# Six weight sets instead of four in an expert loop, its first rows turned earlier, and a tail that reads its two accumulators separately

## The reference

```python
def moe(x, p):                       # 1032 tokens, 64 experts, top 6
    scores = jax.nn.sigmoid(jnp.einsum('nd,de->ne', x, p['w_router']).astype(F32))
    _, e_idx = lax.top_k(scores + p['router_bias'].astype(F32), TOP_K)
    w = jnp.take_along_axis(scores, e_idx, axis=1)
    w = w / jnp.sum(w, axis=-1, keepdims=True) * ROUTED_SCALE
    ...
    shared = swiglu(x, p['w_sh_gate'], p['w_sh_up'], p['w_sh_down'])
    return (routed + shared).astype(x.dtype)   # routed: sum over 6 experts of w * swiglu

x = layer_norm(DN_ALPHA * x + moe(x), ln2_g, ln2_b)
```

## Time and profile before

| | us |
|---|---|
| median of 3 runs | 2173.97 (2173.53 to 2175.95) |
| the profiled execution, device time | 2176.85 |
| its span in the trace | 2175.0 |
| first matmul of the expert loop | 1400.71 |
| first matmul of the last full pair (blocks 62 and 63) | 2088.45 |
| first matmul of the tail | 2134.93 |
| TensorE busy | 2078.7 (96%) |

### The profile page before, as it was taken

The page is one execution under the profiler, slowest core; times in us unless marked ns, Lnnn a source line. Parts: engine busy times, 40 slices in busy tenths (PEclk is TensorE's granted clock), DMA queues, the critical chain, the costliest instruction groups (busy, mean ns, idle before and its releaser), DMA issues.

```text
span 2175.0 us, 28927 instructions
## 1 busy us (share of the span) xinstructions
PE 2078.7 (96%) x10068; PEld 1304.5 (60%) x10068; DVE 1052.0 (48%) x2141; ACT 622.7 (29%) x1326; POOL 634.7 (29%) x782
## 2 busy tenths in 40 slices
PE   7998999899999999999999999999999999999996
PEld 5454665678788888888885556444444444444442
DVE  3225888754476684454444558533333233232335
ACT  1124777555335571121112220011111111111114
POOL 0002665301000000000000000357676656666562
PEclk9998999999999999999999999999999999999998
DMA  8202000347321111022303123699999999999956
GB/s 242 98 1 107 2 2 2 118 154 286 110 54 39 39 36 44 20 59 78 96 21 133 68 89 140 259 351 362 365 359 358 346 354 350 352 363 341 351 166 240
DMA packets 139888, 378.33 MB, mean 174 GB/s; under 512 B 27747, under 2 KB 88887, under 8 KB 112507
## 3 DMA queue, kind: packets, MB, share of 16 engines
q1 hardware_dynamic: 111795, 291.67, 36.5%
q0 software_dynamic: 27120, 84.40, 13.3%
q10 hardware_dynamic: 864, 0.79, 0.1%
HBM read 342.53 MB, written 58.00 MB: 184 GB/s over the span
## 4 chain that ended last, share of the span: by engine, by line
PE 75%; DMA 13%; DVE 5%; ACT 3%; issue 2%; POOL 0%; SPq 0%; DVEq 0%; POOLq 0%; ACTq 0%
PE PS L1277 19%; PE PS L1507 15%; DMA arena<-in_w_exp_down 11%; PE PS L1518 6%; PE PS L917 5%; PE PS L1416 5%; PE PS L806 4%; PE PS L1400 3%; PE PS L950 2%; PE PS L1092 2%; PE PS L987 2%; PE PS L811 2%; PE PS L1580 2%; PE PS L857 1%; PE PS L1455 1%
## 5 line engine op out<-in xcount | busy, mean ns | idle before, releaser
L1277 PE MATMUL PS<-arena 128*128 128x258 f32 x2352 | 514.7, 381 | 3.0 <-DVE arena L2384 2.7
L1507 PE MATMUL PS<-arena 128*128 128x512 f32 x1040 | 462.3, 598 | 30.1 <-issue 14.1
L1277 PEld LDWEIGHTS PS<-arena 128*128 128x128 f32 x2352 | 445.6, 190 | 70.2 <-issue 3.2
L1590 ACT ACTIVATE arena<-PS 128x258 f32<-128x258 f32 (+12 forms) x525 | 237.3, 464 | 656.2 <-PE PS L1277 238.1
L1507 PEld LDWEIGHTS PS<-arena 128*128 128x128 f32 x1040 | 193.7, 191 | 275.0 <-issue 270.0
L2762 POOL DMA_INDIRECT arena<-x_rows,tokall x276 | 278.0, 1007 | 170.6 <-DVE tokall L2615 101.6
L1518 PE MATMUL PS<-arena 128*128 128x512 f32 x520 | 233.9, 592 | 0.5 <-ACT arena L1590 0.5
L2746 POOL MEMSET arena<- 128x2 f32 x1 | 0.1, 100 | 739.8 <-PE PS L1416 739.8
L2636 DVE TENSOR_TENSOR arena<-PS,arena 128x256 f32<-128x256 f32 x65 | 27.6, 425 | 347.7 <-issue 175.6
L1518 PEld LDWEIGHTS PS<-arena 128*128 128x128 f32 x520 | 96.4, 191 | 109.2 <-issue 108.6
L2630 DVE STREAM_TRANSPOSE arena<-arena 128x1024 f32<-128x1024 f32 x67 | 135.7, 2026 | 40.1 <-DMA arena<-x_rows,tokall 39.0
(11 more groups left out here) (344 smaller groups left out, 2266.1 us busy)
## 6 DMA issues: line engine op xcount, KB each, us to landing
arena<-in_w_exp_gate SPq DMA_DIRECT2D x65, 1024.0 KB
arena<-in_w_exp_up SPq DMA_DIRECT2D x65, 1024.0 KB
arena<-in_w_exp_down SPq DMA_DIRECT2D x65, 1024.0 KB
arena<-in_w_in SPq DMA_DIRECT2D x34, 512.0 KB, 5.2
expert_rows<-arena SPq DMA_DIRECT2D x16, 512.0 KB
arena<-expert_rows SPq DMA_DIRECT2D x6, 1024.0 KB, 12.2
arena<-in_x_prompt SPq DMA_DIRECT2D x9, 512.0 KB, 5.0
arena<-x_rows,tokall POOLq DMA_INDIRECT x276
```

What stands on the lines that cost most here:

```text
L1277: ins = mm(PS[:, bank, 0:QT], lhs[:, l0 + k, :], right[:, r0 + k, c0:c0 + QT], start=first and k == 0, stop=k == kh - 1, skip_group_check= ...
L1507: ins = mm(PS[:, 2 + s, :].rearrange("p (h n) -> p h n", h=2), xgT[:, s, k, :], up_w[w][:, :, k, :], start=k == 0, stop=k == KT - 1)
L1590: return fn(out, in_, ACT.Copy)
```

## The change

It has three parts.

**Six weight sets.** Block b uses place b mod 6. The new places lie where constants, routing tables and LN1's vectors lay, whose last readers are done by then. Two of the six (3 and 4) have no room for the last eighth of their up matrix next to the rest, so that piece has a place elsewhere (`up_last`), its own DMA of 1 KB for each partition, and TensorE reads the last slice of gate and up with a longer step (`last_chunk`). The loop on TensorE and SyncE takes three pairs a turn instead of two, with two pairs behind it; a load now waits for the block three pairs earlier. Set 3 is loaded ahead of the loop, set 4 after the last addition, and set 5 where set 3 was.

**Rows of block 0.** VectorE turns the rows of block 0 ahead of the ninth shared addition (8 rows), and TensorE starts block 0 after eight additions.

**Tail.** SyncE reads the second accumulator as soon as `yd1` says that block 63 has been added, and TensorE puts its part of the first four tiles into PSUM; the first accumulator follows after `yd0` into a buffer of its own (`rows1`), and TensorE adds it. In the last full pair GpSimd issues both scatters ahead of the gathers that follow.

The diff, cut to what matters:

```diff
-        up_w = [wex[:, :, 0], wex[:, :, 1], at(4000, 2, KT * DE).rearrange("p h (k n) -> p h k n", k=KT), at(12256, 2, KT * DE).rearrange("p h (k n) -> p h k n", k=KT)]
-        down_w = [wexd[:, 0], wexd[:, 1], at(8096, 2, D), at(16352, 2, D)]
-        s_set = [sem(f"wset{w}") for w in range(4)]
+        NSET, NLATE = 6, 4
+        up_w = [wex[:, :, 0], wex[:, :, 1], gate_up_at(4000), gate_up_at(23536), gate_up_at(P), gate_up_at(12256)]
+        up_last = {3: 29760, 4: 29760 + DE}
+        down_w = [wexd[:, 0], wexd[:, 1], at(8096, 2, D), at(10144, 2, D), at(21472, 2, D), at(16352, 2, D)]
...
-        other = at(30784, NT, D)
+        other = at(12256, NT, D)
+        rows1 = at(30784, NT, D)
...
+            def up_in(w, x):
+                rows = a["w_exp_up"][bass.ds(x, 1), :, :].rearrange("u (p k) n -> (u p) (k n)", p=P)
+                if w in up_last:
+                    sp.dma_start(up_w[w][:, 1, 0:KT - 1].rearrange("p k n -> p (k n)"), rows[:, 0:(KT - 1) * DE]).then_inc(s_set[w], 16)
+                    sp.dma_start(at(up_last[w], DE), rows[:, (KT - 1) * DE:KT * DE]).then_inc(s_set[w], 16)
+                else:
+                    sp.dma_start(up_w[w][:, 1].rearrange("p k n -> p (k n)"), rows).then_inc(s_set[w], 16)
...
+            up_in(3, 3)
             sp.wait_ge(sem("shT_done"), 2)
             down_in(0, 0)
             sp.wait_ge(sem("sh_mm"), 4)
             gate_up_in(2, 2)
             down_in(2, 2)
+            down_in(3, 3)
+            sp.wait_ge(sem("hot_done"), NT)
+            gate_in(3, 3)
             sp.wait_ge(sem("table_step"), 4)
             down_in(1, 1)
...
+            sp.wait_ge(sem("ix1"), 2)
+            sp.wait_ge(sem("set_out"), 16 * NT + 32)
+            gate_up_in(4, 4)
+            sp.wait_ge(sem("shd_mm"), NT)
+            down_in(4, 4)
             sp.wait_ge(sem("x1_out"), 32 * NT)
-            gate_up_in(3, 3)
-            down_in(3, 3)
+            gate_up_in(5, 5)
+            down_in(5, 5)
...
+            def pair_in(r, p):
+                experts = [sp.value_load(blke[0:1, bass.ds(r * NSET + 2 * p + s, 1)], min_val=0, max_val=NE - 1) for s in range(2)]
+                for s, x in enumerate(experts):
+                    sp.wait_ge(sem(f"gu_mm{s}"), r * 3 + p - 1)
+                    gate_up_in(2 * p + s, x)
+                for s, x in enumerate(experts):
+                    sp.wait_ge(sem("y_mm"), r * NSET + 2 * p + s - 3)
+                    down_in(2 * p + s, x)
...
+            sp.wait_ge(sem("yd1"), landed[1])
+            rows_back(other, acc_rows[1], OTHER_IN)
+            sp.wait_ge(sem("yd0"), landed[0])
+            rows_back(rows1, acc_rows[0], Y_IN)
...
-            pe.wait_ge(sem("acc_done"), NT)
+            pe.wait_ge(sem("acc_done"), NT - 1)
...
+            with pe.Fori(0, NE // NSET) as r:
+                for p in range(3):
+                    full(r, p)
+            for p in range(2):
+                full(NE // NSET, p)
...
+            pe.wait_ge(*OTHER_IN[0])
+            for t in range(4):
+                if t == 2:
+                    pe.wait_ge(sem("y_ev"), blocks + 2)
+                    pe.wait_ge(sem("y_ev2"), blocks + 2)
+                sum_of(t, other, False)
             for t in range(NT):
...
+                if t == 4:
+                    pe.wait_ge(*OTHER_IN[4])
+                if t >= 4:
+                    pe.wait_ge(sem("centred"), t - 3)
+                    sum_of(t, other, False)
+                if t in Y_IN:
+                    pe.wait_ge(*Y_IN[t])
+                E.do(sum_of(t, rows1, True), sem("summed"))
...
-            for s in range(2):
-                rows_T(0, s)
+            rows_T(0, 0)
+            shared_add(NT - 1)
+            E.settle()
+            dve.nop().then_inc(sem("y_ev2"), 2)
+            rows_T(0, 1)
+            blocks = dve.value_load(nblk[0:1, 0:1], min_val=NE, max_val=NBLK)
...
+            for s in range(2):
+                rows_out(NE // 2 - 1, s, s)
+            for s in range(2):
+                rows_after_next(NE // 2 - 1, s, 2 + s)
```

More of the change, by code:

```diff
@@ L458, in build @@
         s_const = s_load[4]
-        Y_IN = {m: (s_load[k], (48, 96, 48, 64, 112)[k]) for k, m in enumerate((0, 1, 2, 4, 6))}
+        Y_IN = {m: (s_load[k], (32, 80, 672, 528, 80)[k]) for k, m in enumerate((0, 1, 2, 4, 6))}
         s_x = [sem(f"x_in{k}") for k in range(4)]
         s_xin = s_x[2:4]
+        OTHER_IN = {0: (s_xin[0], 128 + 80 + 16), 4: (s_xin[1], 128 + 64 + 32)}
         s_wta = sem("wta_in")
@@ L761, in spare_in @@
                 down_in(w, x)
[L763 to L771, removed]
+            def pair_in(r, p):
[6 more added lines that the diff above has]
+                    down_in(2 * p + s, x)
+            with sp.Fori(1, NE // NSET) as r:
+                for p in range(3):
+                    pair_in(r, p)
+            for p in range(2):
+                pair_in(NE // NSET, p)
             for lo, hi in SPARE:
@@ L782, in _, with rows_back @@
                                         spare_in(q, 3)
-            for s in range(2):
[L785 to L788, removed]
+            def rows_back(to, rows, groups):
+                for (m, (s, _)), hi in zip(groups.items(), list(groups)[1:] + [NT]):
                     top = min(hi, NT - 1)
@@ L1556, in spare @@
                 down(s, w, 1).then_inc(sem("y_mm"), 1)
-            with pe.Fori(0, NE // 4) as q:
-                for p in range(2):
-                    full(q, p)
+            with pe.Fori(0, NE // NSET) as r:
+                for p in range(3):
+                    full(r, p)
+            for p in range(2):
+                full(NE // NSET, p)
             for lo, hi in SPARE:
@@ L1571, in _, with sum_of @@
                                         spare(q, 3)
-            for t in range(NT):
[L1573 to L1581, removed]
+            def sum_of(t, rows, last):
+                n = rows_of(t)
+                for c in range(2):
+                    ins = mm(PS[0:n, 2 * (t % 4) + c, :], ident[0:n, 0:n], rows[0:n, t, c * 512:(c + 1) * 512], start=not last, stop=last, skip_group_check=True)
+                return ins
+            pe.wait_ge(*OTHER_IN[0])
[4 more added lines that the diff above has]
+                sum_of(t, other, False)
+            for t in range(NT):
+                if t == 4:
[6 more added lines that the diff above has]
+                E.do(sum_of(t, rows1, True), sem("summed"))
         @block.scalar
@@ L2618, in _ @@
                 quarters_of(0, s)
-            for t in range(3, NT):
+            for t in range(3, NT - 1):
                 shared_add(t)
-            for name, n in (("gu_free0", 1), ("gu_free1", 1), ("y_ev2", 2)):
-                dve.nop().then_inc(sem(name), n)
             E.settle()
-            blocks = dve.value_load(nblk[0:1, 0:1], min_val=NE, max_val=NBLK)
+            for name in ("gu_free0", "gu_free1"):
+                dve.nop().then_inc(sem(name), 1)
             def rows_T(i, s):
@@ L2811, in _ @@
             turn(0)
[L2812 removed]
+            with pool.Fori(1, NE // 2 - 1) as i:
                 turn(i)
+            for s in range(2):
+                rows_out(NE // 2 - 1, s, s)
+            for s in range(2):
+                rows_after_next(NE // 2 - 1, s, 2 + s)
             for lo, hi in SPARE:
```

47 lines of the change are left out of this document (31 added, 16 removed).

## The result

The changed kernel takes **2157.14 us** (median of 4 runs, 2155.58 to 2157.3) beside 2174.4 for the kernel before (4 runs, 2173.53 to 2175.95). The ratio is 0.9913, 95% interval 0.99 to 0.9925: 17.3 us less. The forecast was 2159.3 us, 14.7 less, in a range of 2145 to 2167.

A forecast was written before the change was run, and what follows sets the result against it. The prediction took the weight stream (11.3 us a set against TensorE's 10.6) to bound the loop. Loop -9.2 (-8.0, -3.2, +2) and tail -5.5 gave -14.7, from 2173.97 to 2159.3 us, range 2145 to 2167.

The forecast's parts named there:

- The bound: Expert loop: the weight stream limits, not the number of places; weights need 11.3 us a set, TensorE 10.6 a block.
- Rival B: Loop: two more places keep all DMA engines busy, share 1.01 throughout, pair 31 at 2066.2, total -25.7 us; chance 0.17.
- Set 3 early, -8.0: Ahead of the loop: loading set 3 before the accumulator's writes saves its engine time, 7.96 us.
- Sets 4 and 5 at once and the places, -3.2 and 0: Loop start: queuing two sets removes 2.6 us idle, plus 0.6 for an earlier gate load; two more places give 0.
- the 0.6 us for an earlier first load: Loop start: set 4's gate no longer waits for the accumulator's ninth write, so goes out about 0.6 us earlier.
- The split, +2: Loop: 20 sets with split up matrices get 128 extra 1 KB packets each, costing 2 us, bounds 0 and 3.6.
- Block 0, worth 0: Loop start: block 0 starts earlier and without the low clock, 6.8 us, but late weights hide it: worth 0.
- The tail, -5.5: After the last expert block: TensorE begins its sums earlier, 6.4 us less a 0.9 margin; bounds 0 and -10.
- so I say 2128.5: Tail: TensorE's start of the sums put at 2128.5 rather than 2134.93, bounds 2124 and 2134.93.
- the 33.67 us for the records: Tail: TensorE still does all 72 records at the low clock as before, so their 33.67 us stay.
- the 0.9 us taken off for ScalarE and VectorE: Tail: margin of 0.9 us for ScalarE and VectorE falling behind TensorE.
- Rival E: Loop: the longer TensorE body must be fetched, so each of 9 jumps back stalls; slower, 2192 at 6.5 us each; chance 0.05.

The follow-up runs named there:

- the lead of four: Changed kernel with no more than four weight sets in flight in the loop, sets 0 to 5 still asked for ahead of it; ratio 0.9953 to the kernel before.
- the mark: The changed kernel run again with no edit, to compare the follow-up runs against; 2156.3 us, ratio 0.9913 to the kernel before.

## Why the prediction came out as it did

The time, the sign and the place of the gain were right, the time with luck: the loop gave some 5 us more than forecast, the tail some 3 less. The steps:

- **The bound.** "The stream itself is the limit, not the number of places" holds for the lasting pace. In the changed kernel pair 16 starts at 1734.10 and pair 31, 30 sets later, at 2071.31: 11.24 us a set with six places, 11.27 with four. The prediction read the cause as a lasting uneven load, and the run with spread rows bears it out: nothing changed but which partitions hold a block's rows, and the pace went from 11.24 us to something below TensorE's 10.6. The Trainium skill, "DMA: Bandwidth & Descriptors", section "The descriptor swizzle", gives partitions 0 to 63 to engines 0 to 7 and the others to engines 8 to 15; the new placing was built on it. A block has 1032 x 6 / 64 = 97 rows on average. Filled from partition 0, the lower half holds 64 of them and the upper 33. The gain agrees with that rule. That the placing sets the pace is shown; that it does so by way of the engines is inferred, since no view here splits the traffic by engine. The share rose by 4% (0.99 to 1.03) and the bytes by 6% (352 to 374), so engines that stood idle would explain most of the gain and not all. Gathers and scatters got the new placing together; which of them matters was not tried.
- **Rival B** (more places level the load, 1.01 throughout, pair 31 at 2066) fell: from 1650 on the share is 0.99 as before, and the lead of four moves the same bytes there. More lead did raise the rate, but only over the first 100 us.
- **Set 3 early, -8.0**: 8.3 by the profiles, 8 by the timed runs. Choosing engine time over the pace of landing was right.
- **Sets 4 and 5 at once and the places, -3.2 and 0**: together 6.0 (the 0.6 us for an earlier first load gave nothing, so 2.6 became 6.0). This is the term of the loop that was mis-sized. I took a share of 1.01 as full and so counted idle time only in the first 20 us. The same stretch can show 356 GB/s at 1.01 and 376 at 1.03: in the kernel before too few loads were queued for the first 100 us, though TensorE did not yet notice.
- **The split, +2**: 0. Taking a price per packet from a stretch of larger packets invented a cost.
- These make the loop 8.3 + 6.0 = 14.3 us, where 14.6 was measured and 9.2 forecast.
- **Block 0, worth 0**, 6.8 without cover: shown both ways by the profiles, 0.3 us with the weights late and 7.0 with the weights in time (5 by the timed runs).
- **The tail, -5.5**: 2.4 to 3 by the profiles. The failing step is "so I say 2128.5". Reckoned from pair 31, TensorE's sums were to begin 40.05 us later; they begin 42.7 us later, and 43.6 in the mark. The 33.67 us for the records held (35.02 in one execution, 33.28 in the other), and the 0.9 us taken off for ScalarE and VectorE were not needed: from TensorE's last record to the end it is 6.4 to 6.5 us in every profile. The second accumulator's tiles were there 4.35 us before the sums, as the chain shows. What TensorE still lacked was its code, by the packet that ends 1.5 us before the sums; with two of the three jumps gone it starts 2.5 us nearer to its last expert matmul, and the whole tail is 3 to 5 us shorter. I had seen those packets and chosen 2128.5 by guess between the bounds. Whether the fetches are slower because the second accumulator is in flight beside them was not tried.
- **Rival E** fell: no jump back stalls. In the run with spread rows the loop holds 21.2 us a pair to the end.

In the loop the gain was taken too small (5.1 us, of it 2 by the split and 2.8 by the queue), in the tail too large (3). That the sum missed the 17.3 us of the medians by only 2.6 is because the two errors ran against each other.

## What to carry to other kernels

Where gathers and scatters that use only part of the partitions run beside a stream of loads, try spreading their used rows over all partitions. Here that one line was worth 28.8 us on the kernel before (2174.55 to 2145.7), more than the whole change. Judge whether a queue runs full by the bytes moved beside the best stretch of the same traffic, not by a share that looks like 1. And price an edit twice, with its cover and without: block 0's earlier start was worth nothing in the profiles until the weights came in time, and 7 us from then on.

## What the hardware showed that was not expected

With six sets allowed in flight and the weights late, SyncE's own DMA issues become slow. Its issues around 1710 in the timeline of the changed kernel (start us, us of the issue):

```profile
1713.53 8.02 SPq L744 DMA_DIRECT2D arena<-in_w_exp_gate  x1
1721.64 2.97 SPq L753 DMA_DIRECT2D arena<-in_w_exp_up  x1
```

And with the lead of four:

```profile
1708.78 0.33 SPq L744 DMA_DIRECT2D arena<-in_w_exp_gate  x1
...
1709.77 0.33 SPq L751 DMA_DIRECT2D arena<-in_w_exp_up  x1
```

With the lead of four no issue of a weight load behind 1430 takes more than 0.40 us. In the changed kernel half of them take over 2 us and the longest 10.3. It isn't the six places alone: with the rows spread and six places half of them take 0.33 us or less and the longest 2.5. As I read it, the queue takes no more loads from some number on and SyncE stands before it, so that the last places are hardly used, and with the rows spread enough loads have landed by then; no run measures that number. The pace shows no loss by it (352 GB/s either way), since SyncE has little else to do in the loop. What it would cost an engine that issues loads and also computes, no run here shows.
